# A two-block forward pass on one core: every norm split into its parts, and the end worked off by tiles of 128 tokens

## The chip, the cores and the metric

The kernel runs on one core of a Trainium2 chip. The metric is the device time of one execution in microseconds (us). Engines are named as in the profile: PE is the TensorE matmul engine (PEld its weight loads), DVE is VectorE, ACT is ScalarE, POOL is GpSimd, SP the engine that only issues DMAs.

## The reference

All is float32, for 512 tokens of width 1024. A first block runs on x, a second on the result. What touches the change are the norms between the products, and the end:

```python
def rms_norm(x, g):
    y = x * lax.rsqrt(jnp.mean(x * x, axis=-1, keepdims=True) + EPS)
    return y * g
# first block
h = rms_norm(x, g_pre_mix);  proj = h @ w_in                    # stage in1
mem_kv = rms_norm(mem, g_mem) @ w_mem_kv
y = concat(rms_norm(y_attn), rms_norm(y_conv), rms_norm(y_x)) @ w_out   # out1
x = x + rms_norm(y, g_post_mix)
f = square(relu(rms_norm(x, g_pre_mlp) @ w_up)) @ w_down        # up, down
x = x + rms_norm(f, g_post_mlp)
# second block: h = rms_norm(x) * (1 + scale) + shift; the same for 256 context rows
lat, ctx = h_lat @ w_in_2, h_ctx @ w_in_2                       # in2q, in2
q = rms_norm(lat[0]) @ w_q_b;  kv = rms_norm(lat[1], ctx[1]) @ w_kv_b   # mla0q ...
...                                  # attention, a gated scan, out, router
# expert layer: each token's 4 expert rows, weighed and added, then
x = x + gate * sum(prob[k] * expert_row[k] for k in range(4))
out = rms_norm(x, final_norm_g)
```

## The kernel before, in words

Activations lie transposed: the partitions hold 128 features, a tensor of width 1024 is eight chunks of 128 x 512 tokens. A product stage (`products`, L849) takes weight tiles of 1 MB that SP has queued, and works on pairs of output chunks: eight input chunks by eight matmuls of 512 columns, then ACT evacuates the pair from its banks (L1351). A float32 matmul is two records in the trace. There are only two sets of banks for pairs, so PE's third pair needs ACT to have emptied the first.

Each engine runs its own written-out program, in order, and waits on semaphores. A norm is a chain over four engines. DVE squares the chunks into two buffers `sq` (L1606), PE sums the squares over the partitions with a matrix of ones (`norm`, L910), ACT takes the root (`norm_root`, L1358), DVE inverts it (L1613), PE spreads the result over the partitions (`norm_spread`, L920), DVE multiplies chunk after chunk by it (L1619). Before the change PE's program holds sums and spread as one block between two product stages. Those blocks stand:

- ahead of `in1` for `pre_mix` and then `mem`; ACT's program goes on behind the root of `mem` with two sines for the rotary angles, a load of another function table and a sigmoid (L1393 to L1397), and only then evacuates `in1`. DVE computes the angles behind its own part of the norm of `mem`;
- ahead of `out1` for `attn`, `conv`, `xattn`, one after another; behind `out1` for `post_mix`, whose result is added to x chunk by chunk (L1730, L1731), and then for `pre_mlp`, whose squares DVE takes when all additions are done; likewise `post_mlp` and `mix2` behind `down`;
- between `in2q` and `in2` for `ctx`, behind `in2` for `qin`, `ckv_lat` and `ckv_ctx`, with the rotation of the keys, and then `mla0q`.

The expert layer runs 84 blocks of 32 rows: `up` L1238, `down` L1260, weight tiles of 1 MB queued on SP into 20 slots (two of them in the buffer of x), and a store of each block's 128 KB of results on ACT's queue. The last block stands in a loop of its own (`Fori`), since its count is only known at run time; ahead of it DVE waits for the store of the third block from the end, and then picks the last block's biases. During the expert layer x is kept in memory, since its buffer serves as weight slots; SP loads it back (`x<-x_kept`) when the last block's `down` is done. Then POOL gathers the expert rows by 16 indirect DMAs of 128 rows, four for each tile of 128 tokens (L811). DVE weighs and adds the four rows of a tile (L2030, L2033), PE transposes the sum (L1323), ACT copies it (L1584), DVE scales it and adds it to x (L2018, L2019). When all four tiles are in x the norm `final` runs over all of x, and SP stores eight chunks (L733).

## Time and profile before

| | |
|---|---|
| median of 3 runs | 3381.93 us (3380.32 to 3383.77) |
| the profiled execution's own time | 3386.95 us |
| its span | 3384.9 us, mean granted clock 0.93 |
| PE, PEld busy | 89%, 46% |
| DVE, ACT, POOL busy | 29%, 19%, 6% |
| DMA | 585 MB, 173 GB/s over the span |

The span runs from the first to the last event of the profiled execution; 2.05 us of its time lie around the span. The busy shares are means over the whole span. PE is at nine tenths in nearly all of the page's 40 slices; it is the stretches in which it isn't that the change is about.

### The profile page before, as it was taken

The page shows a single profiled execution, that of the slowest core. Times are in us where ns is not written, and L with a number is a line of the kernel's source. Part 1 is how long each engine was busy: PE and PEld are TensorE (multiplying, and loading weights), DVE is VectorE, ACT ScalarE, POOL GpSimd, SP SyncE. Part 2 cuts the span into 40 slices and gives each one's busy share as a digit, 9 for nine tenths or more (in the row PEclk, how much of TensorE's full clock was granted, in tenths as well). Part 3 has the DMA queues.
Part 4 walks back from the last instruction along what each step waited for, and adds up shares of the span by engine and source line. Part 5 has one row for each costly group of instructions (what it writes and reads, how often), then busy time and mean ns, then how long its engine had stood idle before and what let it go on. Part 6 is the DMA issues. An engine that isn't in the chain of part 4 may idle for free.

```text
span 3384.9 us, 45853 instructions
## 1 busy us (share of the span) xinstructions
PE 3014.4 (89%) x19729; PEld 1551.5 (46%) x19729; DVE 980.2 (29%) x1988; ACT 652.4 (19%) x1345; POOL 190.3 (6%) x180
## 2 busy tenths in 40 slices
PE   6899879999888999889999896799899999999993
PEld 3554434444344666555666664433333333333331
DVE  2244130000222221444445545411122121111124
ACT  1133000000001333344334332110111111111101
POOL 0000000000000000111111111110000000000002
PEclk9998889999888999899999998799999999999996
DMA  3134212211201011511011110398999979999695
GB/s 150 50 150 174 87 47 78 75 62 50 100 27 35 27 44 41 196 44 44 19 44 44 44 38 0 133 414 339 414 375 385 418 311 418 401 386 392 263 380 217
DMA packets 116909, 585.12 MB, mean 173 GB/s; under 512 B 10244, under 2 KB 21540, under 8 KB 69860
## 3 DMA queue, kind: packets, MB, share of 16 engines
q1 hardware_dynamic: 92752, 536.14, 40.0%
q10 hardware_dynamic: 17652, 24.25, 2.0%
q0 software_dynamic: 6304, 21.80, 1.8%
q8 instruction: 156, 2.56, 0.3%
q14 instruction: 45, 0.37, 0.0%
HBM read 551.58 MB, written 30.57 MB: 172 GB/s over the span
## 4 chain that ended last, share of the span: by engine, by line
PE 77%; DMA 10%; DVE 8%; ACT 2%; issue 1%; SPq 1%; ACTq 0%; POOL 0%; DVEq 0%; POOLq 0%
PE product_banks L849 37%; PE product_banks L1238 14%; PE product_banks L1260 8%; DMA space<-in_wgu 6%; PE score_banks L1132 3%; DMA x<-in_wgu 2%; PE out_bank L1000 1%; PE out_bank L920 1%; PE score_banks L937 1%; PE out_bank L959 1%; SPq L713 1%; PE turn_bank L910 1%; PE product_banks L1157 1%; DVE sq L1606 1%; PE product_banks L836 1%
## 5 line engine op out<-in xcount | busy, mean ns | idle before, releaser
L849 PE MATMUL product_banks<-space 128*128 128x512 f32 (+2 forms) x3888 | 1384.0, 508 | 32.3 <-DVE space L1832 13.4
L849 PEld LDWEIGHTS product_banks<-space 128*128 128x128 f32 x3888 | 687.2, 196 | 613.0 <-issue 552.2
L1238 PE MATMUL product_banks<-space 128*32 128x512 f32 x4848 | 581.5, 613 | 56.3 <-DMA space<-in_wgu 56.3
L1238 PEld LDWEIGHTS product_banks<-space 128*32 128x32 f32 x4848 | 141.0, 111 | 373.7 <-issue 266.6
L1260 PE MATMUL product_banks<-space,rstd 128*32 128x256 f32 x5024 | 300.7, 392 | 1.2 <-ACT rstd L1545 1.2
L1967 DVE TENSOR_TENSOR sq<-product_banks,cst 128x512 f32<-128x512 f32 x85 | 58.8, 692 | 755.4 <-PE product_banks L1238 755.4
L1351 ACT ACTIVATE space<-product_banks 128x512 f32<-128x512 f32 (+1 forms) x226 | 110.1, 523 | 796.1 <-PE product_banks L849 776.6
L1260 PEld LDWEIGHTS product_banks<-space,rstd 128*32 128x32 f32 x5024 | 168.4, 114 | 162.3 <-issue 73.4
L762 POOL TENSOR_TENSOR space<-space 128x512 f32<-128x512 f32 x112 | 132.0, 1193 | 1033.0 <-ACT space L1484 932.7
L1132 PE MATMUL score_banks<-space 128*128 128x64 f32 x896 | 126.3, 289 | 27.3 <-issue 21.1
L1132 PEld LDWEIGHTS score_banks<-space 128*128 128x128 f32 x896 | 124.6, 212 | 42.1 <-issue 38.3
L1606 DVE TENSOR_TENSOR sq<-space 128x512 f32<-128x512 f32 (+1 forms) x58 | 33.0, 605 | 375.5 <-PE turn_bank L910 237.9
L1541 ACT ACTIVATE ms<-sq 128x256 f32<-128x256 f32 x85 | 35.4, 417 | 459.3 <-DVE sq L1970 459.3
L910 PE MATMUL turn_bank<-sq,cst 128*32 128x128 f32 (+1 forms) x784 | 47.1, 337 | 79.8 <-DVE sq L1606 78.4
L1545 ACT ACTIVATE rstd<-turn_bank 128x256 f32<-128x256 f32 x85 | 32.7, 384 | 365.8 <-PE turn_bank L1249 365.8
L1238 PE MATMUL product_banks<-x,space 128*32 128x512 f32 x592 | 76.2, 628 | 7.1 <-DMA x<-in_wgu 7.1
L1853 DVE COPY_PREDICATED space<-cst,score_banks 128x256 f32<-128x256 uint8 x112 | 58.3, 520 | 67.7 <-PE score_banks L1132 67.0
L1738 DVE TENSOR_TENSOR space<-space 128x1024 f32<-128x1024 f32 x16 | 19.6, 1226 | 200.0 <-ACT space L1351 200.0
L1861 DVE TENSOR_TENSOR space<-space 128x256 f32<-128x256 f32 x112 | 69.5, 620 | 12.8 <-ACT space L1501 12.8
L784 POOL DMA_INDIRECT cst<-h_rows,space x21 | 20.0, 954 | 923.0 <-PE score_banks L1227 917.5
L910 PEld LDWEIGHTS turn_bank<-sq,cst 128*32 128x32 f32 x784 | 18.0, 124 | 115.0 <-DVE sq L1606 81.1
L1981 DVE TENSOR_TENSOR zeros<-product_banks,cst 128x256 f32<-128x256 f32 x84 | 35.7, 425 | 120.8 <-PE product_banks L1260 113.2
(300 smaller groups left out, 2476.3 us busy)
## 6 DMA issues: line engine op xcount, KB each, us to landing
space<-in_wgu SPq DMA_DIRECT2D x230, 1024.0 KB, 21.7
space<-in_wdn SPq DMA_DIRECT2D x116, 1024.0 KB, 21.9
space<-in_wt SPq DMA_DIRECT2D x104, 1024.0 KB, 5.1
x<-in_wgu SPq DMA_DIRECT2D x26, 1024.0 KB, 23.1
y_rows<-zeros ACTq DMA_DIRECT2D x2, 6400.0 KB, 29.5
x<-in_wdn SPq DMA_DIRECT2D x12, 1024.0 KB, 23.5
y_rows<-zeros ACTq DMA_DIRECT2D x84, 128.0 KB
space<-in_wt SPq DMA_DIRECT2D x13, 512.0 KB, 4.5
```

Of the source, the lines that this page charges most:

```text
L762: gp.tensor_tensor(dlt[:, L % 2, 0:T].rearrange("p (b s) -> p b s", s=2 * hf), c3, ref.broadcast_to([P, nb, 2 * hf]), ALU.subtract).then_i ...
L849: ins = nc.tensor.matmul(bank[0:rows, at:at + cols], lhsT, rhs, start=(i == 0), stop=(i == len(mm) - 1))
L910: ins = nc.tensor.matmul(PT[ROWS * q:ROWS * q + ROWS, 0:w // 4], ones[:, 0:ROWS], sq[:, g % 2, w // 4 * q:w // 4 * (q + 1)], start=(c == 0 ...
L1132: ins = nc.tensor.matmul(LB[L % 2][:, 64 * c:64 * c + 64], X[:, L % 2, cs_], half, start=True, stop=True)
L1238: ins = nc.tensor.matmul(bank[ROWS * g:ROWS * g + ROWS, :], xT_[:, k, :], w[:, 512 * g:512 * g + 512], start=(k == 0), stop=(k == DC - 1))
L1260: ins = nc.tensor.matmul(bank[ROWS * g:ROWS * g + ROWS, :], aT_[:, P * c + ROWS * d:P * c + ROWS * d + ROWS], w[:, c, 256 * g:256 * g + 25 ...
L1351: ins = nc.scalar.activation(dst, src, func, bias=bias, scale=scale)
L1606: V.tensor_tensor(sq[:, g % 2, 0:w], src[:, c, 0:w], src[:, c, 0:w], ALU.mult).then_inc(s_sq, 1)
L1853: V.copy_predicated(to, mk, LB[L % 2][:, 0:256].rearrange("p (c b s) -> p c b s", c=TT, s=hf)).then_inc(s_at, 1)
L1861: V.tensor_tensor(xv[:, :, qh], ev[:, :, qh], views(qq, hf)[:, :, qh], ALU.mult)
L1967: V.tensor_tensor(tbuf, bank, bias[:, 0:512], ALU.add).then_inc(s_u, 1)
L1981: V.tensor_tensor(to, bank, bias[:, 512:768], ALU.add).then_inc(s_y, 1)
```

## The change

**Norms.** `mem`'s sums and spread move into the stream of `in1` (behind 16 and 32 matmuls), `ctx`'s into that of `in2q`, `qin`'s into that of `in2`, those of `ckv_lat` and `ckv_ctx`, with the key rotation, into `mla0q` behind 18 matmuls. `attn`, `conv` and `xattn` are done abreast: all squares, all sums, all roots, all inversions, all spreads. A product stage behind a norm starts with the first chunk that is multiplied, not with the last. The squares of an output are summed within the stage that makes it (`products_and_sums`). The squares of `pre_mlp` and `mix2` are taken by ACT, chunk by chunk as DVE adds (`residual_squares`). x is loaded first, and the constants in two parts.

**x back.** `x<-x_kept` is queued ahead of the last block's tiles, which go to other slots.

**The end.** All 16 gathers have buffers of their own. For each tile ACT weighs the first row (`weigh_first`), DVE adds the second and third, and PE transposes that sum into a bank by a product with the identity and adds the fourth row there by a product with the identity times the row's weights. DVE adds the bank, times the gate, to x. The norm and the stores run per tile as well: ACT squares, PE sums with a full 128 x 128 matrix of ones (which also spreads), ACT takes the root and multiplies by the gain, DVE inverts and multiplies, SP stores 512 KB.

```diff
-            sp.dma_start(cst[:, :], consts).then_inc(s_const, 16)
+            sp.dma_start(x, xT).then_inc(s_in, 16)
+            sp.dma_start(cst[:, 0:2 * P], consts[:, 0:2 * P]).then_inc(s_unit, 16)
             sp.dma_start(vec[:, :], vecs).then_inc(s_const, 16)
-            sp.dma_start(x, xT).then_inc(s_in, 16)
+            sp.dma_start(cst[:, 2 * P:N_CONST], consts[:, 2 * P:N_CONST]).then_inc(s_const, 16)
...
+                for i in range(NS_SPACE, NS):
+                    sp.wait_ge(*released[i + NS * (loads_of_slot[i] - 1)])
+                sp.dma_start(x, xkept).then_inc(s_xback, 16)
...
-                sp.wait_ge(s_dn, n_more + N_FIXED_BLOCKS)
-                sp.dma_start(x, xkept).then_inc(s_xback, 16)
...
+                for i in range(TT):
+                    sp.wait_ge(s_fin, i + 1)
...
+            def products_and_sums(stage, name, source=None):
+                size = products_in(stages[stage][0])
+                for i, _ in enumerate(product_steps(stage)):
+                    if source and i < DC - 1:
+                        pe.wait_ge(s_norm, source + i + 1)
+                    p, done = divmod(i + 1, size)
+                    if p >= 2 and done == DC:
+                        norm_sum(name, 2 * p - 4)
+                        norm_sum(name, 2 * p - 3)
+                for c in range(4, DC):
+                    norm_sum(name, c)
...
-            norm("mem")
-            norm_spread("mem")
...
-            products("in1", "pre_mix")
+            for i, _ in enumerate(product_steps("in1")):
+                if i < DC - 1:
+                    pe.wait_ge(s_norm, normed("pre_mix", i + 2))
+                if i == 2 * DC - 1:
+                    norm("mem")
+                if i == 4 * DC - 1:
...
-            norm("attn")
-            norm_spread("attn")
-            norm("conv")
-            norm_spread("conv")
-            norm("xattn")
-            norm_spread("xattn")
-            pe.wait_ge(s_norm, normed("xattn"))
-            products("out1")
-            norm("post_mix")
+            for name in ("attn", "conv", "xattn"):
+                norm(name)
+            for name in ("attn", "conv", "xattn"):
...
-            products("in2q", "mix2")
-            norm("ctx")
-            norm_spread("ctx")
-            pe.wait_ge(s_norm, normed("ctx"))
-            products("in2")
-            norm("qin")
-            norm_spread("qin")
+            for i, _ in enumerate(product_steps("in2q")):
+                if i < DC - 1:
+                    pe.wait_ge(s_norm, normed("mix2", i + 2))
+                if i == 2 * DC - 1:
+                    norm("ctx")
+                if i == 4 * DC - 1:
+                    norm_spread("ctx")
+            for i, _ in enumerate(product_steps("in2")):
+                if i == 2 * DC - 1:
+                    norm("qin")
+                    pe.wait_ge(s_norm, normed("ctx"))
+                if i == 4 * DC - 1:
+                    norm_spread("qin")
             norm("ckv_lat")
-            norm_spread("ckv_lat")
             norm("ckv_ctx")
-            norm_spread("ckv_ctx")
-            pe.wait_ge(s_evac, stages["in2"][1])
-            rope(8)
-            pe.wait_ge(s_norm, normed("ckv_ctx"))
-            products("mla0q")
+            pe.wait_ge(s_norm, normed("qin"))
+            for i, _ in enumerate(product_steps("mla0q")):
+                if i == 17:
+                    norm_spread("ckv_lat")
+                    norm_spread("ckv_ctx")
+                    pe.wait_ge(s_evac, stages["in2"][1])
+                    rope(8)
+                    pe.wait_ge(s_norm, normed("ckv_ctx"))
             pe.wait_ge(s_evac, stages["mla0q"][1])
             rope(9)
             for g in range(4):
...
+            def sum_squares(i):
+                pe.wait_ge(s_fsq, i + 1)
+                if i:
+                    pe.wait_ge(s_frt, i)
+                for c in range(DC):
+                    ins = nc.tensor.matmul(PT[:, 0:P], ones, squares[:, i % 2, P * c:P * c + P], start=(c == 0), stop=(c == DC - 1))
+                ins.then_inc(s_fmm, 1)
...
+                bank = row_banks[i % 2]
+                pe.wait_ge(s_acc, 2 * i + 2)
+                if i >= 2:
+                    pe.wait_ge(s_xt, i - 1)
                 for c in range(DC):
-                    ins = nc.tensor.transpose(S[:, P * c:P * c + P], acc[:, i, P * c:P * c + P], ident)
-                ins.then_inc(s_tT, 1)
-            norm("final")
-            norm_spread("final")
+                    nc.tensor.matmul(bank[:, P * c:P * c + P], acc[:, i, P * c:P * c + P], ident, start=(c % 4 == 0), stop=False)
+                if i >= 2:
+                    sum_squares(i - 2)
+                j = TOPK * i + 3
+            sum_squares(TT - 2)
+            sum_squares(TT - 1)
...
+            def residual_squares(name, added):
+                for c in range(DC):
+                    g = chunk0[NI[name]] + c
+                    act.wait_ge(s_xadd, added + c + 1)
+                    act.wait_ge(s_mm, g - 1)
+                    nc.scalar.activation(sq[:, g % 2, :], x[:, c, :], F.Square).then_inc(s_sq, 1)
...
+            def weigh_first(i):
+                j = TOPK * i
+                act.wait_ge(*yg_landed(j))
+                nc.scalar.activation(acc[:, i, :], yg[:, j, :], F.Copy, scale=prob[:, j:j + 1]).then_inc(s_y0, 1)
+
+            act.wait_ge(s_weigh, 1)
+            for i in range(3):
+                weigh_first(i)
             for i in range(TT):
-                act.wait_ge(s_tT, i + 1)
-                nc.scalar.activation(yT[:, :, P * i:P * i + P], v3(S[:, :], DC), F.Copy).then_inc(s_tTc, 1)
-            norm_root("final")
+                ts = slice(P * i, P * i + P)
+                act.wait_ge(s_xt, i + 1)
+                if i >= 2:
+                    act.wait_ge(s_fmm, i - 1)
+                nc.scalar.activation(v3(squares[:, i % 2, :], DC), x[:, :, ts], F.Square).then_inc(s_fsq, 1)
+                if i == 0:
+                    weigh_first(3)
+                for c in range(DC):
+                    ins = nc.scalar.activation(fin[:, c, ts], x[:, c, ts], F.Copy, scale=vcol("final_norm_g_2", c))
+                ins.then_inc(s_gain, 1)
+                act.wait_ge(s_fmm, i + 1)
+                nc.scalar.activation(ms[:, ts], PT[:, 0:P], F.Sqrt, bias=const("eps"), scale=1.0 / D).then_inc(s_frt, 1)
...
+            def add_two(i):
+                dve.wait_ge(s_y0, i + 1)
+                for j in (TOPK * i + 1, TOPK * i + 2):
+                    dve.wait_ge(*yg_landed(j))
+                    if j % TOPK == 2:
+                        dve.wait_ge(s_acc, 2 * i + 1)
+                    V.scalar_tensor_tensor(acc[:, i, :], yg[:, j, :], prob[:, j:j + 1], acc[:, i, :], ALU.mult, ALU.add).then_inc(s_acc, 1)
+
+            def finish(i):
+                dve.wait_ge(s_frt, i + 1)
+                link(V.reciprocal(rstd[:, ts], ms[:, ts]))
+                dve.wait_ge(s_gain, i + 1)
```

PE's program at the start, before. The names are output and inputs; L910 sums squares, L920 spreads, L849 is `in1`; x counts matmuls.

```order
L910 MATMUL turn_bank<-sq,cst 32x128 x32
L920 MATMUL out_bank<-rstd,cst 128x128 x4
L910 MATMUL turn_bank<-sq,cst 32x64 x32
L920 MATMUL out_bank<-rstd,cst 128x64 x4
L849 MATMUL product_banks<-space 128x512 x64
L849 MATMUL product_banks<-space 128x256 x64
```

The same place after the change (L947 sums, L957 spreads, L874 is `in1`).

```order
L947 MATMUL turn_bank<-sq,cst 32x128 x32
L957 MATMUL out_bank<-rstd,cst 128x128 x4
L874 MATMUL product_banks<-space 128x512 x16
L947 MATMUL turn_bank<-sq,cst 32x64 x32
L874 MATMUL product_banks<-space 128x512 x16
L957 MATMUL out_bank<-rstd,cst 128x64 x4
L874 MATMUL product_banks<-space 128x512 x32
L874 MATMUL product_banks<-space 128x256 x64
```

The sums of `mem` stand behind the first pair of `in1`, its spread behind the second. ACT's program beside it, after the change, from its start; the row with `ms` and 64 is the root of `mem`, L1414 evacuates `in1`.

```order
L1423 ACTIVATE ms<-turn_bank,cst 128x128
L1423 ACTIVATE ms<-turn_bank,cst 128x64
L1466 ACT_TABLE_LOAD
L1466 ACTIVATE space<-space 128x512
L1468 ACTIVATE space<-space 128x512
L1470 ACT_TABLE_LOAD
L1470 ACTIVATE small<-vec 128x16
L1414 ACTIVATE space<-product_banks 128x512 x8
```

Nothing moved on ACT: no evacuation stands ahead of root, sines and sigmoid. The second place is PE's program from `in2` to `mla0q`, before.

```order
L849 MATMUL product_banks<-space 128x256 x8
L910 MATMUL turn_bank<-sq,cst 32x128 x24
L920 MATMUL out_bank<-rstd,cst 128x128 x4
L910 MATMUL turn_bank<-sq,cst 32x128 x8
L920 MATMUL out_bank<-rstd,cst 128x128 x4
L910 MATMUL turn_bank<-sq,cst 32x64 x8
L920 MATMUL out_bank<-rstd,cst 128x64 x4
L929 MATMUL score_banks<-space,cst 128x512
L849 MATMUL product_banks<-space 128x512 x20
```

And after the change.

```order
L947 MATMUL turn_bank<-sq,cst 32x128 x24
L874 MATMUL product_banks<-space 128x256 x16
L957 MATMUL out_bank<-rstd,cst 128x128 x4
L874 MATMUL product_banks<-space 128x512 x8
L874 MATMUL product_banks<-space 128x256 x8
L947 MATMUL turn_bank<-sq,cst 32x128 x8
L947 MATMUL turn_bank<-sq,cst 32x64 x8
L874 MATMUL product_banks<-space 128x512 x18
L957 MATMUL out_bank<-rstd,cst 128x128 x4
L957 MATMUL score_banks<-rstd,cst 128x64 x4
L966 MATMUL score_banks<-space,cst 128x512
```

Sums and spread of `qin` (x24, then x4) now have products of `in2` between them, and the two other norms have 18 matmuls of `mla0q`. The third place is DVE's program in the end, after the change: L2140 adds a gathered row, L2153 adds a tile to x, L2145 and L2147 finish a tile's norm.

```order
L2140 SCALAR_TENSOR_TENSOR space<-space 128x1024 x4
L2153 SCALAR_TENSOR_TENSOR x<-score_banks,mod,x 128x128 x8
L2140 SCALAR_TENSOR_TENSOR space<-space 128x1024 x2
L2153 SCALAR_TENSOR_TENSOR x<-product_banks,mod,x 128x128 x8
L2140 SCALAR_TENSOR_TENSOR space<-space 128x1024 x2
L2145 RECIPROCAL rstd<-ms 128x128
L2147 TENSOR_TENSOR space<-space,rstd 128x8x128
L2153 SCALAR_TENSOR_TENSOR x<-score_banks,mod,x 128x128 x8
L2145 RECIPROCAL rstd<-ms 128x128
L2147 TENSOR_TENSOR space<-space,rstd 128x8x128
L2153 SCALAR_TENSOR_TENSOR x<-product_banks,mod,x 128x128 x8
```

Before, four additions and two operations on x stood for each tile, and all of the norm behind the last; now a tile takes two additions, eight small ones and its own two steps of the norm.

## Rows read from the trace of the kernel before

**Rows 1.** Page, part 4: the chain that ended last, by engine.
```profile
PE 77%; DMA 10%; DVE 8%; ACT 2%; issue 1%; SPq 1%; ACTq 0%; POOL 0%; DVEq 0%; POOLq 0%
```

**Rows 2.** PE's waits over the span: waited for, us in total, times, longest us.
```profile
PE turn_bank L910 <- DVE sq L1606: 78.4, 46, 18.7
```

**Rows 3.** DMA issues of the span: KB each, median us to landing.
```profile
x<-x_kept SPq DMA_DIRECT2D x1, 2048.0 KB, 7.8
outT<-space SPq DMA_DIRECT2D x8, 256.0 KB, 2.2
cst<-in_consts SPq DMA_DIRECT2D x1, 1718.0 KB, 9.0
```

**Rows 4.** Timeline, 20 to 45 us: start, us, engine line op, idle before it.
```profile
27.93 5.35 DVE L1619 SCALAR_TENSOR_TENSOR space<-x,vec,out_bank 128x512 f32<-128x512 f32 x8 [2.17 <-PE out_bank L920]
```

**Rows 5.** ACT's timeline, 48 to 60 us.
```profile
51.00 1.28 ACT L1397 ACT_TABLE_LOAD   x1
...
56.45 1.08 ACT L1351 ACTIVATE space<-product_banks 128x512 f32<-128x512 f32 x2 [3.94 <-PE product_banks L849]
```

**Rows 6.** Chain in order of time, 0 to 690 us: start, us, what.
```profile
1.78 16.03 DMA x<-in_xT
...
40.40 84.86 PE product_banks L849 x256
...
460.93 221.82 PE product_banks L849 x512
```

**Rows 7.** Timeline, 346 to 373 us: the norms ahead of out1.
```profile
349.16 2.60 DVE L1606 TENSOR_TENSOR sq<-space 128x512 f32<-128x512 f32 x4
...
352.83 0.95 DVE L1613 RECIPROCAL rstd<-ms 128x128 f32<-128x128 f32 x1 [1.08 <-ACT ms L1358]
...
353.84 2.07 PE L920 MATMUL out_bank<-rstd,cst 128*128 128x128 f32 x8 [1.46 <-DVE rstd L1613]
...
372.55 1.22 PE L849 MATMUL product_banks<-space 128*128 128x512 f32 x1 [1.50 <-DVE space L1619]
```

**Rows 8.** Timeline, 449 to 457 us: the norm pre_mlp.
```profile
450.13 1.29 DVE L1606 TENSOR_TENSOR sq<-x 128x512 f32<-128x512 f32 x2
...
456.60 0.37 ACT L1358 ACTIVATE ms<-turn_bank,cst 128x128 f32<-128x128 f32 x1 [21.69 <-PE turn_bank L910]
```

**Rows 9.** Timeline, 982 to 1056 us: norms behind in2q and in2.
```profile
982.99 0.43 PE L910 MATMUL turn_bank<-sq,cst 128*32 128x64 f32 x16
...
995.65 33.61 PE L849 MATMUL product_banks<-space 128*128 128x512 f32 x96 [6.42 <-DVE space L1754]
...
1029.19 0.65 PE L910 MATMUL turn_bank<-sq,cst 128*32 128x128 f32 x16
...
1052.89 3.42 PE L849 MATMUL product_banks<-space 128*128 128x512 f32 x5
```

**Rows 10.** Timeline, 680 to 690 us: PE behind an idle stretch, at down.
```profile
685.17 5.40 PE L849 MATMUL product_banks<-space 128*128 128x512 f32 x8 [2.44 <-DVE space L1738]
```

**Rows 11.** Chain in order of time, 3280 to 3330 us.
```profile
3283.84 15.05 DMA y_rows<-zeros
...
3320.32 8.33 DMA y_rows<-conditions
```

**Rows 12.** Line 811 alone: the gathers, DMA to landing.
```profile
DMA to landing us min/median/max: 4.4/6.1/6.5
```

**Rows 13.** Groups of instructions, DVE by shape: busy us, mean ns.
```profile
L1642 DVE SCALAR_TENSOR_TENSOR space<-score_banks,cst 128x128 f32<-128x128 f32 x8 | 2.3, 291 | 3.9 <-PE score_banks L937 3.6
```

**Rows 14.** Timeline, 3349 to 3367 us: the end.
```profile
3350.00 1.77 POOL L811 DMA_INDIRECT space<-y_rows,space  x1 [0.30 <-issue]
...
3357.02 4.06 DVE L2033 SCALAR_TENSOR_TENSOR space<-space 128x1024 f32<-128x1024 f32 x3
...
3361.14 1.97 PE L1323 MATMUL score_banks<-cst,space 128*128 128x128 f32 x8 [5.38 <-DVE space L2033]
...
3363.14 1.02 ACT L1584 ACTIVATE space<-score_banks 128x1024 f32<-128x1024 f32 x1 [6.33 <-PE score_banks L1323]
```

## What I predict, and why

> **What bounds the kernel now.** I read the page from the busy shares and the slices to the chain that ended last, and then the waits. PE carries 77% of that chain, DMA 10%, DVE 8% [rows 1]: time is to be had where PE stands still or runs at half clock. The waits of PE name the place: it waits 78.4 us for DVE's squares, in 46 waits [rows 2]. A norm between two product stages keeps PE nearly idle, and the stage behind it begins at the lower level of the granted clock: the ordinary 512-column record takes 221.82 / 512 = 0.433 us [rows 6], the first eight of `down` take 5.40 us, 0.675 each [rows 10], the first of `out1` 1.22 [rows 7]. So one idle stretch costs about 5.40 - 8 x 0.433 = 1.9 us beside its own length. What bounds the end is in rows 14: the last gather is issued at 3350.0, it lands 6 us later [rows 12], and the span ends 28.9 us behind that, at 3384.9.
>
> **The start: 1 us lost.** x is issued at 1.78 and lands at 17.8, behind 1.7 MB of constants [rows 6]; those take 9.0 us [rows 3], so 2 MB first in the queue take 9.0 x 2048 / 1718 = 10.7 and land at about 11.4, 6.4 earlier. The first multiplication follows from 27.93 [rows 4] to 21.5, the first matmul of `in1` comes one chunk later, at 22.2, not at 40.40 [rows 6]. That is 18.2 us. What is given back: `mem`'s sums in the stream, 3.4 (a group of 16 such records takes 0.43 at full clock [rows 9] and there are four; I take twice that, for the gaps around each chunk's group), and its spread, 1.0 (half of the 2.07 of rows 7, at full clock). And a wait that the order of ACT's program makes. PE's third pair needs the first evacuated. On ACT the evacuation stands behind the root of `mem`, the two sines, the table load and the sigmoid, the sines wait for DVE's angles, and those stand behind DVE's norm of `mem`, which waits for the spread. The spread is now behind pair 1: 22.2 + 16.05 (40.40 to 56.45 for pair 0 [rows 5, 6]) + 3.4 + 32 x 0.433 + 1.0 is 56.5. From the spread's end to the sigmoid's it was 40.40 to 52.5 (the table load from 51.00 to 52.3 [rows 5], 0.2 for the sigmoid), with the evacuation's 1.08 it is 13.2 us, in which PE has nothing. It costs 2.0 of clock again. `in1` ends at 22.2 + 84.9 + 3.4 + 1.0 + 13.2 + 2.0 = 126.7 against 125.3: **-1.4**. The bounds are no such wait (+13.8), and a wait with 3 us more of slow records (-4).
>
> **Attn, conv, xattn: +10.7.** Before it is 349.16 to 372.55, 23.4 us [rows 7]. Now eight squares in a row, 0.65 each, to 354.4; the last sums and root 1; three inversions of 0.95 [rows 7], the first two beside the spreads; three spreads of 2.07 back to back end at about 363, where the attn chunks have long been multiplied, and `out1` starts: 9.5, and 1.2 of clock, since PE has just worked 6 us.
>
> **post_mix to pre_mlp, and post_mlp to mix2: +5.5 each.** DVE squares from 450.13 on, the root is at 456.60 [rows 8], 6.5 us. Now ACT squares each chunk while DVE multiplies the next, and behind the last addition stand one square and four matmuls: 1.0. The two have the same shape. The sums of post_mix within the stage may give up to 1.5 more each; none would be left if the additions waited for ACT. I take nothing for it.
>
> **ctx: +8.7.** It is 982.99 to 995.65, 12.7 us, and the 96 records behind it take 33.61 [rows 9] where 48 of 0.433 and 48 of half that make 31.2: 15.1 in all. In the stream it costs 3.4 for the sums, 1.0 for the spread, and some 2 of gaps.
>
> **qin and ckv: +12.** It is 1029.19 to 1052.89, 23.7 us [rows 9]. Now `qin`'s sums cost 3.7 (24 x 2 records, 0.65 for 16 [rows 9], and gaps), its spread 1.0, the ckv sums 1.7, their spreads and the rotation 3.4, and the restart 2: 11.8. What covers ACT's and DVE's part are the 18 matmuls of `mla0q` (15.6 us); if `qin` were late, PE would wait in front of them, up to 4.
>
> **x back ahead of the last block: +0.9.** The last block's tiles are now behind 2 MB: 7.8 less the 2.2 that even 256 KB take [rows 3], 5.6, less 1.2 that its last tile is asked for earlier: -4.4. Gained is the last store's landing, 8.33 beside the load of x [rows 11], about 3 alone: +5.3. The bounds: the store of which DVE waits ahead of the last block took 15.05 [rows 11] and may take more with the copy beside it (-4); the copy hidden beside stores gives +3. The Trainium skill (DMA: Bandwidth & Descriptors, Queues, rings and completion order) says that each DMA engine takes turns between queue rows packet by packet, so a small store on another queue should not stand behind all that SP has queued. The trace shows 15.05 us for 128 KB under load; the page would make this item about +1.5.
>
> **The end: +8.5.** The gathers keep their pace. Behind the last landing DVE owes the finish of tile 0, tile 2's addition, the finish of tile 1 and tile 3's addition, each about 2.3 (eight additions of 0.291 [rows 13]; 0.95 and 1.35), 9; then ACT's square 1.0 (as the copy of rows 14), the sums 2, root 0.4, inversion 0.95, multiplication 1.35 (a third of 4.06 [rows 14]) and a store of 512 KB, 3: 17.7, and about 2.7 between engines: 20.4 against 28.9. This wants PE at full clock. The matrices of a tile are three times 16 records; 8 of them took 1.97 us at half clock [rows 14], so a tile takes 12 us there, four tiles 47 from the second landing on, and the end comes some 18 later: **-9**. PE has more to do than before, and doesn't stop; I take the upper case, with both as bounds. The table load, 1.28 [rows 5], is once on the path in both kernels, and ACT goes on at once behind it. By the Trainium skill (ScalarE: Activation LUTs, What ACT_TABLE_LOAD costs) a switch costs 2.66 us with its drain; that would change the end by 1.4 at most.
>
> **The sum:** -1.4 + 10.7 + 5.5 + 5.5 + 8.7 + 12 + 0.9 + 8.5 = 50.4. The profiled execution has 3386.95 us, 2.05 more than its span and 5.0 more than the median; the change would take it to 3336.6. From the median of 3381.93 it is 3331.5, and I say **3332**.
>
> **Rivals.** (a) All as above, chance 0.60, own range 3322 to 3342. (b) No wait in `in1`, since the angles don't wait for the spread or the evacuation comes first: the start gains 13.8, 3317; against it stands the order of ACT's rows. 0.08. (c) The clock falls at each norm that now stands in a stream, and in the end: five places by 2 us and half of the end's 18, 18 to 20 us less: 3350. For it: the clock falls already at waits of some us [rows 10]. 0.17. (d) The two copies and the end give nothing, since DVE's additions are bound by the landings and the stores by the queue: 9.4 less, 3341. 0.12. (e) On the other side: after the short waits that each stage now has, the clock stays at its lower level for the product stages themselves. A 512-column record then takes 0.85 (1.22 and less were seen only in the first few [rows 7]); each costs 0.42 more, and 120 of them eat the 50 us, out of 3888. From 130 on it is slower. `in1`'s first pair, 32 records in 16.05 us [rows 5, 6], shows that such a stretch is possible; that it ends there speaks against it. 3385 to 3400, 0.02. The rest, 0.01, is no change.
>
> **How the numbers follow.** The unknown costs add to about 10 us either way: the end -17.5 or +2.5, the start +15, the copy -5 or +2, the others 4. The range 3314 to 3348 takes in (a), (b) and (d) and most of (c). A measurement of this kernel can tell 0.2%, 7 us, from no change. Faster by more: 0.97; within it: 0.01; slower: 0.02.
>
> **What the profile of the changed kernel would show.** Step one: `in1`'s first matmul near 22, PE idle for some 13 us near 57, until ACT's first evacuation near 70; right after a sigmoid. If that idle stretch is missing, (b) is right. Out1's first matmul is 14 us behind the first square of attn. PE has no idle stretch of 12 us between `in2q` and `mla0q`. The gap from the last addition of post_mix to the root of pre_mlp is near 1.5. The last store of a block lands 3 us after issue, the last block's `down` ends some 4 us later than its queue alone would have it. In the end PE's records of 128 columns take 0.12 us, not 0.25, and the span ends about 20 us behind the last landing. The prediction is wrong by most if the clock in the page's slices is lower than before in the middle of the stages, or if the PE of the end is at half.

## The result, and the profile after

The changed kernel takes 3329.39 us (median of 4 runs, 3322.44 to 3333.18) against 3381.12 for the kernel before beside it: the ratio is 0.9847, 95% interval 0.9834 to 0.9859, or 52 us less. The profiled execution has 3331.52 us and a span of 3329.8, 55.1 below that of before. Here is the page after: the span, PE's busy time, and the chain that ended last by engine.

```profile
span 3329.8 us, 46098 instructions
...
PE 3017.5 (91%) x19817; PEld 1561.9 (47%) x19817; DVE 952.9 (29%) x1975; ACT 681.7 (20%) x1408; POOL 188.9 (6%) x180
...
PE 79%; DMA 9%; DVE 6%; ACT 3%; another core or an unknown queue 1%; issue 1%; ACTq 0%; SPq 0%; POOL 0%; DVEq 0%; POOLq 0%
```

PE's share of the chain rose from the 77% of [rows 1] to 79%, DVE's fell from 8% to 6%. The waits of PE after (waited for, us in total, times, longest) answer to [rows 2].

```profile
PE product_banks L874 <- ACT space L1414: 19.4, 8, 13.1
...
PE turn_bank L947 <- ACT sq L1430: 14.7, 16, 2.2
...
PE turn_bank L947 <- DMA cst<-in_consts: 13.5, 1, 13.5
...
PE turn_bank L947 <- DVE sq L1706: 9.9, 23, 1.8
```

Of the 78.4 us of waiting for DVE's squares 9.9 are left, and 14.7 for the squares that ACT now takes. Two long waits are to be read beside them: a new one of 13.1 us for ACT to empty the product banks, and one of 13.5 us for constants at the start.

**Where the time went.** A product stage's evacuations on ACT are the same in number and order in both kernels, so the difference of their start times is a running balance. It makes this table (us; in the balance minus is earlier than before; "this part" is what the stretch up to that place gained, minus is a loss; of the 85 expert blocks 84 stand ahead of the loop).

| place | before | after | balance | this part | forecast |
|---|---|---|---|---|---|
| in1, last pair emptied | 125.28 | 131.23 | +5.95 | -5.95 | -1.4 |
| out1, last pair | 429.41 | 425.36 | -4.05 | +10.0 | +10.7 |
| up, first pair | 476.77 | 465.26 | -11.51 | +7.5 | +5.5 |
| in2q, first pair | 955.63 | 934.20 | -21.43 | +9.9 | +5.5 |
| in2, first pair | 1012.08 | 979.68 | -32.40 | +11.0 | +8.7 |
| mla0q, once spreads and rotation are done | 1071.36 | 1025.70 | -45.66 | +13.3 | +12 |
| last block but one, up done | 3287.43 | 3236.93 | -50.50 | +4.8 | 0 |
| first gather | 3329.56 | 3280.87 | -48.69 | -1.8 | +0.9 |
| end of the span | 3384.9 | 3329.8 | -55.1 | +6.4 | +8.5 |

**The start.** The timeline of the changed kernel, 10 to 75 us (start, us, engine line op, in brackets the idle time before it and what ended it).

```profile
13.51 1.08 PE L947 MATMUL turn_bank<-sq,cst 128*32 128x128 f32 x16 [13.51 <-DMA cst<-in_consts]
...
19.29 1.28 ACT L1423 ACT_TABLE_LOAD   x1 [19.29 <-PE turn_bank L947]
...
24.91 16.99 PE L874 MATMUL product_banks<-space 128*128 128x512 f32 x32 [0.84 <-DVE space L1724]
...
58.85 1.00 PE L957 MATMUL out_bank<-rstd,cst 128*128 128x64 f32 x8
...
59.89 3.22 DVE L1724 SCALAR_TENSOR_TENSOR space<-space,vec,out_bank 128x256 f32<-128x256 f32 x8 [13.84 <-PE out_bank L957]
...
69.29 0.63 ACT L1466 ACTIVATE space<-space 128x512 f32<-128x512 f32 x1 [22.52 <-DVE space L1793]
69.82 0.61 ACT L1468 ACTIVATE space<-space 128x512 f32<-128x512 f32 x1
70.45 1.28 ACT L1470 ACT_TABLE_LOAD   x1
71.75 0.21 ACT L1470 ACTIVATE small<-vec 128x16 f32<-128x16 f32 x1
71.87 2.04 ACT L1414 ACTIVATE space<-product_banks 128x512 f32<-128x512 f32 x4
...
72.99 2.93 PE L874 MATMUL product_banks<-space 128*128 128x512 f32 x3 [13.13 <-ACT space L1414]
```

PE starts at 13.51, released by the constants and not by x, which DVE squares from 10.51 on. ACT's first table load, 1.28 us, comes only at 19.29, behind the last sum, so that the root of `pre_mix` stands 1.3 us later behind the sums than before. In the kernel before it ran at the very start, beside the loads:

```profile
0.87 1.28 ACT L1358 ACT_TABLE_LOAD   x1 [0.87 <-PEq L2131]
```

The changed program has ACT wait for the constants ahead of this root; that this is what put the load there is likely, but no run tests it. PE reaches `in1` at 24.91 and spreads `mem` at 58.85. Then the chain can be read downward: DVE applies the norm of `mem` (59.89), computes the angles, ACT takes the sines (69.29), loads a table (70.45), runs the sigmoid (71.75), and only then empties the first pair (71.87), which had been ready since 41.9. PE's third pair starts at 72.99 after 13.13 us of idle time. That answers to [rows 5], where the same rows stood before PE had need of them.

**The three norms ahead of out1.** The chain in order of time, 355 to 375 us.

```profile
363.19 2.08 PE out_bank L957 x8
365.26 3.41 PE score_banks L957 x16
368.68 6.60 PE product_banks L874 x15
```

The three spreads stand back to back and `out1` starts right behind them, 13.0 us behind the first square (355.68) where it was 23.4 [rows 7].

**Squares on ACT.** The timeline at `pre_mlp`: the last square, the root, `up`.

```profile
442.51 0.63 ACT L1430 ACTIVATE sq<-x 128x512 f32<-128x512 f32 x1 [0.75 <-PE turn_bank L947]
...
443.92 0.37 ACT L1423 ACTIVATE ms<-turn_bank,cst 128x128 f32<-128x128 f32 x1 [0.78 <-PE turn_bank L947]
...
448.31 4.63 PE L874 MATMUL product_banks<-space 128*128 128x512 f32 x5 [0.84 <-DVE space L1724]
```

DVE's last addition ends at 442.5, the root comes 1.4 us later, where the squares alone took 6.5 [rows 8]. At `post_mlp`:

```profile
898.20 0.37 ACT L1423 ACTIVATE ms<-turn_bank,cst 128x128 f32<-128x128 f32 x1 [1.87 <-PE turn_bank L947]
...
899.61 1.16 PE L957 MATMUL out_bank<-rstd,cst 128*128 128x128 f32 x8 [1.47 <-DVE rstd L1717]
```

The root is 3.0 us behind the evacuation of 895.24, not 4.9, and the spread takes 1.16 us, not the 2.07 of [rows 7]: PE has hardly stopped, and its clock is still up.

**Norms in the stream.** The timeline from 934 to 1000 us, `ctx` and `qin`.

```profile
937.28 14.00 PE L874 MATMUL product_banks<-space 128*128 128x512 f32 x32
...
951.12 1.00 PE L957 MATMUL out_bank<-rstd,cst 128*128 128x64 f32 x8
...
983.15 8.86 PE L874 MATMUL product_banks<-space 128*128 128x256 f32 x32
...
991.85 1.05 PE L957 MATMUL out_bank<-rstd,cst 128*128 128x128 f32 x8
```

Each spread is 1.0 us between products that run on, behind `ctx` at 0.44 a record of 512 columns; what stood between the stages in [rows 9] is not there. Behind the sums of `qin` the 32 records of 256 columns take 8.86 us, in e7, e11 and e12 7.17: here the clock did fall in the stream, for 1.7 us.

**The copies and the end.** DMA issues over the span (KB each, us to landing), which answer to [rows 3]:

```profile
x<-in_xT SPq DMA_DIRECT2D x1, 2048.0 KB, 9.6
...
cst<-in_consts SPq DMA_DIRECT2D x1, 128.0 KB, 12.1
```

x lands after 9.6 us, but the 128 KB of constants queued behind it only after 12.1. And the end, from the store of the last block:

```profile
3276.59 1.09 ACTq L1631 DMA_DIRECT2D y_rows<-conditions  x1
3280.12 0.18 POOL L806 TENSOR_TENSOR space<-space 1x1 f32<-1x1 f32 x1 [111.31 <-DMA y_rows<-conditions]
...
3316.11 1.95 PE L1370 MATMUL turn_bank<-space,cst 128*128 128x128 f32 x16
3317.05 2.15 DVE L2153 SCALAR_TENSOR_TENSOR x<-product_banks,mod,x 128x128 f32<-128x128 f32 x8
...
3319.24 1.06 ACT L1678 ACTIVATE space<-x 128x1024 f32<-128x1024 f32 x1 [0.77 <-DVE x L2153]
...
3320.35 2.85 PE L1370 MATMUL turn_bank<-space,cst 128*128 128x128 f32 x16 [2.29 <-ACT space L1678]
...
3324.62 1.23 DVE L2147 TENSOR_TENSOR space<-space,rstd 128x1024 f32<-128x1024 f32 x1
```

POOL goes on 3.5 us after the store is issued, not 8.3 [rows 11]. Tile 3 is added at 3317.05, squared at 3319.24, and its sums take 2.85 us for 16 records, where those of tile 2 just ahead (3316.11) take 1.95: the granted clock fell once more. The last two windows of the span show where it stood (busy us and count by engine, granted clock, DMA share, GB/s).

```profile
3281.00:3300.00 19.00, 8.97 (x62) 8.81 (x63) 6.27 (x9) 3.44 (x3) 14.62 (x15) 0.66 0.90 332
3300.00:3330.00 30.00, 17.71 (x133) 17.03 (x131) 20.81 (x40) 17.18 (x42) 0.95 (x1) 0.80 0.42 140
```

### The profile page after: what moved, and what is told of

Read it like the earlier page. It is cut to its first block, busy times and chain, and to the rows that moved or that the text cites. A ratio compares the mean times of both kernels' runs of the same rounds, so it can differ in the third digit from the quotient of the medians.

```text
span 3329.8 us, 46098 instructions
## 1 busy us (share of the span) xinstructions
PE 3017.5 (91%) x19817; PEld 1561.9 (47%) x19817; DVE 952.9 (29%) x1975; ACT 681.7 (20%) x1408; POOL 188.9 (6%) x180
## 4 chain that ended last, share of the span: by engine, by line
PE 79%; DMA 9%; DVE 6%; ACT 3%; another core or an unknown queue 1%; issue 1%; ACTq 0%; SPq 0%; POOL 0%; DVEq 0%; POOLq 0%
PE product_banks L874 37%; PE product_banks L1284 14%; PE product_banks L1306 8%; DMA space<-in_wgu 6%; PE score_banks L1178 3%; DMA x<-in_wgu 2%; PE out_bank L1037 1%; PE score_banks L974 1%; PE out_bank L996 1%; PE product_banks L1203 1%; PE turn_bank L947 1%; PE product_banks L861 1%; PE out_bank L957 1%; DMA space<-in_wdn 1%
## 5 line engine op out<-in xcount | busy, mean ns | idle before, releaser
L874 PE MATMUL product_banks<-space 128*128 128x512 f32 (+2 forms) x3888 | 1383.4, 508 | 39.0 <-ACT space L1414 19.4
L874 PEld LDWEIGHTS product_banks<-space 128*128 128x128 f32 x3888 | 686.1, 196 | 614.0 <-issue 547.4
L1284 PE MATMUL product_banks<-space 128*32 128x512 f32 x4864 | 583.8, 614 | 55.3 <-DMA space<-in_wgu 52.4
L1414 ACT ACTIVATE space<-product_banks 128x512 f32<-128x512 f32 (+1 forms) x226 | 109.9, 522 | 767.0 <-PE product_banks L874 745.3
L947 PE MATMUL turn_bank<-sq,cst 128*32 128x128 f32 (+1 forms) x720 | 39.6, 315 | 39.5 <-ACT sq L1430 14.7
L1582 ACT ACTIVATE space<-space 128x256 f32<-128x256 f32 x112 | 47.3, 423 | 118.6 <-DVE space L1980 118.6
L2099 DVE TENSOR_TENSOR zeros<-product_banks,cst 128x256 f32<-128x256 f32 x84 | 35.7, 425 | 121.5 <-PE product_banks L1306 112.6
```

Of the source, the lines that this page charges most:

```text
L874: ins = nc.tensor.matmul(bank[0:rows, at:at + cols], lhsT, rhs, start=(i == 0), stop=(i == len(mm) - 1))
L947: ins = nc.tensor.matmul(PT[ROWS * q:ROWS * q + ROWS, at:at + w // 4], ones[:, 0:ROWS], sq[:, g % 2, w // 4 * q:w // 4 * (q + 1)], start=( ...
L1284: ins = nc.tensor.matmul(bank[ROWS * g:ROWS * g + ROWS, :], xT_[:, k, :], w[:, 512 * g:512 * g + 512], start=(k == 0), stop=(k == DC - 1))
L1414: ins = nc.scalar.activation(dst, src, func, bias=bias, scale=scale)
L1582: nc.scalar.activation(ev[:, :, qh], dv[:, :, qh], F.Exp)
L2099: V.tensor_tensor(to, bank, bias[:, 512:768], ALU.add).then_inc(s_y, 1)
```

## Experiments

All times below are medians, with the ratio to the kernel before from the same chip and its 95% interval. The changed kernel's own profiled execution stood at a lower clock in some stretches than those of the experiments, so that most of them are up to 3 us ahead of it at places that their edit does not touch; at the end of `in1` the seven that leave the start alone are 0.1 to 2.3 us ahead. So a difference of that size counts for nothing by itself: a balance is read across the stage that was edited, and where that isn't enough, by the rows at the place. The medians of e7, e8 and e12 lie 5.7 to 6.1 us above that of the changed kernel, where the balance moves by 9.5 to 11.2 at the edited stage; where the rest goes isn't resolved.

**e1: pairs of in1 emptied ahead of the sines.**

```diff
             norm_root("mem")
+            evacuate_to(stages["in1"][0] + 2)
             act.wait_ge(s_ang, 1)
```

> The changed kernel, but ACT empties the first two pairs of in1 ahead of the sines, the table load and the sigmoid. If PE's 13.3 us of idle time behind the spread of mem come from that order, they go, and with them some 2 us of half clock behind them: in1 ends 13 to 15 us earlier and the time is about 3315 (ratio to before 0.980 to 0.981). If PE would wait there anyway, for a weight tile or for DVE, the time stays at 3329 within 3 us.

Measured: 3310.77 us, ratio 0.9792 (0.9776 to 0.9808). The timeline at the place:

```profile
58.50 1.09 ACT L1414 ACTIVATE space<-product_banks 128x512 f32<-128x512 f32 x2 [12.61 <-PE product_banks L874]
...
59.14 16.10 PE L874 MATMUL product_banks<-space 128*128 128x512 f32 x37
```

ACT empties pair 1 at 58.50, PE's products start 0.6 us after and don't stop (37 records in 16.10, 0.435 each). `in1` ends 16.8 us earlier than in the changed kernel, and at the end of `out1` it is 18.0. The wait is ACT's order. By the rows it costs 13.3 us between the two records beside it, and 2.9 of half clock behind it (the first eight records take 6.38 us in the changed kernel and 3.48 here); the other 0.5 arises ahead of it, in `in1`'s first records, where the edit changes nothing.

**e2: angles ahead of the norm of mem.** DVE's eleven instructions for the angles stand ahead of `norm("mem", hm, "g_mem")`; ACT is as in the changed kernel.

```diff
-            dve.wait_ge(s_tok, 16)
-            norm("mem", hm, "g_mem")
             dve.wait_ge(s_pos, 16)
             link(V.tensor_copy(cosT, ang.bitcast(i32)))
...
             V.tensor_scalar(trn, trn, PI, -PI, ALU.min, ALU.max).then_inc(s_ang, 2)
+            dve.wait_ge(s_tok, 16)
+            norm("mem", hm, "g_mem")
```

> The changed kernel, but DVE computes the rotary angles ahead of its part of the norm of mem, so that sines and sigmoid do not stand behind the spread; ACT's order is as in the changed kernel. If the link from the spread over DVE's angles to the sines makes the wait, it goes here as fully as by the other order on ACT: 3315. If ACT's order alone matters, whatever DVE does (table loads and sines behind the root of mem), some 2 to 5 us of the wait stay: 3317 to 3320.

Measured: 3308.86 us, 0.9779 (0.9762 to 0.9797); the first evacuation is at 49.25 instead of 71.87, `in1` ends 16.3 us earlier. Breaking the chain at either link removes all of it.

**e3: the first constants ahead of x.**

```diff
-            sp.dma_start(x, xT).then_inc(s_in, 16)
             sp.dma_start(cst[:, 0:2 * P], consts[:, 0:2 * P]).then_inc(s_unit, 16)
+            sp.dma_start(x, xT).then_inc(s_in, 16)
```

> The changed kernel, but the first 256 columns of the constants are loaded ahead of x, not behind it. PE waited for them until 13.5 us, when x had been there since 10.5. They are 128 KB; x should land about 0.5 us later and PE start at about 11.5: 2 us less, all of it on the path, 3327 (the timing alone may not tell that, the time of the first matmul will). If small loads are late because of the other loads that start at once, and not because of their place, the first matmul stays near 13.5 and nothing is gained.

Measured: 3321.55 us, 0.9822 (0.9805 to 0.9838). The first rows of DVE and PE:

```profile
11.18 1.29 DVE L1706 TENSOR_TENSOR sq<-x 128x512 f32<-128x512 f32 x2 [9.79 <-DMA x<-in_xT]
...
12.02 1.17 PE L947 MATMUL turn_bank<-sq,cst 128*32 128x128 f32 x16 [12.02 <-DVE sq L1706]
```

x lands 0.7 later (11.18), PE starts 1.5 earlier, and `in1` starts 1.5 earlier (23.41; 24.6 to 25.0 in the others that load x first). That is what the edit is worth. The balance of 1.8 to 2.1 at the evacuations doesn't show more, since executions without the edit are up to 2.3 ahead there. The place in the queue is what counted. The time fell by 8 us; that surplus lies in the stretches that differ between any two profiled executions, and I don't put it down to the edit.

**e4: mem ahead of in1 again.**

```diff
             norm_spread("pre_mix")
+            norm("mem")
+            norm_spread("mem")
             pe.wait_ge(s_norm, normed("pre_mix", 1))
...
-                if i == 2 * DC - 1:
-                    norm("mem")
-                if i == 4 * DC - 1:
-                    norm_spread("mem")
```

> The changed kernel, but sums and spread of mem stand ahead of in1 again, as in the kernel before. in1 starts about 12.5 us later, near 37, sums and spread (4.3 us) and the 13.3 us of waiting go from its stream, and with them 2 us of half clock: in1 ends 7 to 9 us earlier than with mem in the stream, 3321. If the wait for ACT were there in either place, in1 would end 12 us later than in the changed kernel: 3341.

Measured: 3316.48 us, 0.9799 (0.9778 to 0.9821); `in1` ends 11.0 us earlier, 9.5 at the end of `out1`. Undone, this part is faster than done. Against e1, which keeps `mem` in the stream, it loses 5.8 us at the one place and 8.5 at the other.

**e5: x loaded back last.**

```diff
-                for i in range(NS_SPACE, NS):
-                    sp.wait_ge(*released[i + NS * (loads_of_slot[i] - 1)])
-                sp.dma_start(x, xkept).then_inc(s_xback, 16)
...
+                sp.wait_ge(s_dn, n_more + N_FIXED_BLOCKS)
+                sp.dma_start(x, xkept).then_inc(s_xback, 16)
                 for i in range(TT):
                     sp.wait_ge(s_fin, i + 1)
```

> The changed kernel, but x is loaded back as before, when the last block's down is done, behind its tiles. By the prediction the copy ahead of the block was worth 0.9 us, so this is 0.9 slower. By the trace of the changed kernel the last block's up ends 4.7 us later against the blocks ahead of it, its down 6.8, and the last store lands 4.8 earlier: undone it is 1.8 to 2 us faster. In the trace: last store near 8 us to landing instead of 3.5, and the last block's first addition 4.7 earlier. The timing can hardly tell either; the trace's boundaries can.

Measured: 3326.33 us, 0.9838 (0.9824 to 0.9852), against the changed kernel unclear. The parts can be read. The expectation compared two executions in which the stream of weight tiles stood one tile (2.7 us) apart against PE, though the code of the expert layer is the same: with the copy first, `up` of the last block is done 28.0 to 28.2 us behind that of the block ahead of it in six of the profiled executions, 24.7 to 26.0 in six others. The phase shows elsewhere too: the six others and the kernel before lose 2.6 to 3.3 us between expert blocks 76 and 78 that the first six don't lose, and e5 doesn't, so it belongs with the first six. Like with like: from `up` of the block ahead to the last store 39.7 us with the copy first, 35.7 with it last (and 37.3 in e1 against 32.9 before, in the other phase). That is 4.0 to 4.4 us. From the store to the first gather 4.3 against 9.4: 5.1. The copy's place is worth +1.2 to +0.5 us from `up` to the first gather. The expectation here was wrong, the prediction right.

**e6: tiles before finishes, on PE and DVE.**

```diff
+                if i == 3:
+                    sum_squares(0)
...
+            for i in range(1, TT):
+                sum_squares(i)
...
-            finish(0)
             add_tile(2)
-            finish(1)
+            finish(0)
             add_tile(3)
+            finish(1)
```

> The changed kernel, but in the end PE turns tile 3's sum ahead of the squares of tile 0 and sums the squares of tile 1 behind tile 3's fourth row, and DVE adds tiles 2 and 3 to x one finish earlier each. In the changed kernel tile 3's addition starts at 3317.05, 0.8 us after PE is done with it, and PE is done late since it sums squares before. If DVE and PE together bound the end, the last store is issued about 2 us earlier, the end is 2 us shorter from the first gather on (46.9 instead of 48.9). If the end is bound by the landings of the rows, nothing changes.

Measured: 3329.02 us, 0.9843 (0.9829 to 0.9858). From the first gather to the end 46.9 us, in the ten executions with the end as changed (the changed kernel, e1 to e5, e7, e8, e11, e12) 45.7 to 48.9, median 46.6. Nothing gained, and neither of the two explanations holds: the rows (ACT, DVE, ACT) show a third.

```profile
3304.75 0.37 ACT L1685 ACTIVATE ms<-turn_bank,cst 128x128 f32<-128x128 f32 x1 [3.17 <-PE turn_bank L1370]
...
3307.28 2.15 DVE L2153 SCALAR_TENSOR_TENSOR x<-product_banks,mod,x 128x128 f32<-128x128 f32 x8
...
3312.12 1.05 ACT L1678 ACTIVATE space<-x 128x1024 f32<-128x1024 f32 x1
```

Tile 3 is added 32.3 us behind the first gather (36.2 in the changed kernel, 34.0 in e8), but ACT squares the next tile only behind the root and the gains of the last one: the squares of tile 3 begin at 3312.12, 2.7 us after its addition has ended. And ACT is late at its first root (3304.75) since the edit itself makes PE sum tile 0's squares behind tile 3's sum: it waits 3.17 us there, and from then on squares, gains and root of the other three tiles follow one another without a break, 3.55 us for each.

**e7: ctx between the stages again.** The root stands behind all of `in2q`'s evacuations, too.

```diff
-                if i == 2 * DC - 1:
-                    norm("ctx")
-                if i == 4 * DC - 1:
-                    norm_spread("ctx")
+            norm("ctx")
+            norm_spread("ctx")
+            pe.wait_ge(s_norm, normed("ctx"))
```

> The changed kernel, but the norm of ctx stands between in2q and in2 again, as a block. The prediction said 8.7 us for this part; the two traces, by the evacuations of in2q and in2, say 11.0. So it is slower by 8.7 or by 11: 3338 or 3340. If the two figures differ because the clock's level behind the block was not what it was, the trace shows it in the first records of in2.

Measured: 3335.35 us, 0.9863 (0.9846 to 0.988). At the first pair of `in2` it has lost 11.2 us (its balance against the changed kernel goes from -0.2 to +11.05), at the second 9.4 is left, and in the expert layer 6.4 to 9.2 from its tenth block on. The part is worth 11, and 6 to 9 of it stays.

**e8: squares by DVE.**

```diff
-            residual_squares("pre_mlp", 0)
-            residual_squares("mix2", DC)
...
-            inverse_root("pre_mlp")
+            norm_stats("pre_mlp")
...
-            inverse_root("mix2")
+            norm_stats("mix2")
```

> The changed kernel, but DVE squares the new x for pre_mlp and for mix2 itself, behind its additions; all else (sums of the output within its stage, the shift on ACT) as changed. By the prediction the squares on ACT are worth 5.5 us each, 11 in all: 3340. If the 8.6 to 9.1 us that these two gaps lost come mostly from the squares, more than 14 is given back; I expect 5.7 each from the rows (last addition to root 7.1 before, 1.4 now), 11.4.

Measured: 3335.13 us, 0.9865 (0.9848 to 0.9882). The balance moves by 4.2 us at `pre_mlp` and 5.9 at `mix2`, 10.1.

**e9: the fourth row by DVE.**

```diff
-                for j in (TOPK * i + 1, TOPK * i + 2):
+                for j in (TOPK * i + 1, TOPK * i + 2, TOPK * i + 3):
...
-                pe.wait_ge(*yg_landed(j))
-                for c in range(DC):
-                    ins = nc.tensor.matmul(bank[:, P * c:P * c + P], yg[:, j, P * c:P * c + P], weigh[:, i, :], start=False, stop=(c % 4 == 3))
```

> The changed kernel, but the fourth row is added by DVE like the second and third, and PE only transposes the sum; the rest of the end stays by tiles. It gives DVE 1.34 us more for each tile and takes 16 records, 2.0 us, from PE. If DVE bounds the end, from the first gather to the end it takes 47.5 instead of 46.2 (the median of the eight profiled executions with this end); if PE does, 44. The rest of the run is not touched.

PE also turns the sum by 8 records a tile instead of 16 here (`transpose` in place of the product with the identity), so that it loses 24 records a tile and not 16.

Measured: 3330.61 us, 0.984 (0.9825 to 0.9856). From the first gather to the end 48.1 us, 1.5 more than the median of the ten executions with the changed end, but within their 45.7 to 48.9. So a gain, the 44 us of the case that PE bounds the end, is excluded; a loss isn't shown by one execution. The windows of its end, and of e2's, which has the changed end:

```profile
3282.00:3301.00 19.00, 3.91 (x16) 3.13 (x16) 9.75 (x15) 3.44 (x3) 15.01 (x14) 0.50 0.88 308
3301.00:3330.00 29.00, 12.02 (x80) 11.15 (x80) 22.19 (x39) 17.25 (x42) 2.99 (x3) 0.74 0.47 160
```

```profile
3260.00:3279.00 19.00, 8.56 (x60) 8.41 (x61) 8.09 (x13) 4.40 (x4) 14.77 (x14) 0.64 0.88 309
3279.00:3306.00 27.00, 16.09 (x134) 15.09 (x132) 19.08 (x36) 16.02 (x42) 2.65 (x3) 0.97 0.52 172
```

DVE does 32 us of work, not 27, and PE, with 80 records instead of 134 in the last stretch, runs at a granted clock of 0.74, not 0.97. Over the last 29 us of the ten executions with the changed end it is 0.80 to 0.96, and in the kernel before, with 104 records in the whole end, 0.50. So with less work PE stood at a lower clock; what that costs in time isn't shown, since DVE's own 5 us more lie beside it.

**e11: sums of the outputs behind their stages.**

```diff
-                    if p >= 2 and done == DC:
-                        norm_sum(name, 2 * p - 4)
-                        norm_sum(name, 2 * p - 3)
-                for c in range(4, DC):
+                for c in range(DC):
                     norm_sum(name, c)
```

> The changed kernel, but all squares of the outputs of out1 and down are summed behind the stage, not within it. I had taken nothing for that part; the traces say that from the last evacuation to the root it was 5.1 and 4.9 us and is 3.0, that the spread behind it then still runs at the upper clock (1.6 and 1.2 us instead of 2.07), and that the sums cost 1.5 in the stream. So 1 to 2.5 us are given back in the two places together: 3330 to 3332, and in the trace the first additions of post_mix and post_mlp come 0.5 to 1.3 us later each. If nothing was gained by it, the boundaries stay within 0.3.

Measured: 3329.87 us, 0.9838 (0.9823 to 0.9853). The stages without sums are 1.5 us shorter each; at `up` 1.9 of it is given back again, at `in2q` 3.8. So the part is worth 0.4 at `post_mix` and 2.3 at `post_mlp`. The rows at `post_mlp`:

```profile
896.29 0.37 ACT L1420 ACTIVATE ms<-turn_bank,cst 128x128 f32<-128x128 f32 x1 [4.06 <-PE turn_bank L944]
...
897.69 2.08 PE L954 MATMUL out_bank<-rstd,cst 128*128 128x128 f32 x8 [1.48 <-DVE rstd L1714]
```

The root is 5.2 us behind the evacuation of 891.14, and the spread takes 2.08 us, at half clock. Behind `qin`'s sums this execution gets 1.7 back without an edit there:

```profile
982.84 7.17 PE L874 MATMUL product_banks<-space 128*128 128x256 f32 x32
```

**e12: attn, conv, xattn one after another.**

```diff
             for name in ("attn", "conv", "xattn"):
                 norm(name)
-            for name in ("attn", "conv", "xattn"):
                 norm_spread(name)
```

On DVE, which the cut doesn't show, squares and inversion of each norm stand together again, and each root waits for its own sums alone.

> The changed kernel, but attn, conv and xattn are normed one after another again, each with its squares, sums, root, inversion and spread; out1 still starts as soon as its first input chunk and the last spread are there. Before, from the first square to the last spread's end it took 21.9 us, in the changed kernel 13.0 to the first matmul: 8.9 more, and 1 to 2 of half clock in out1's first records behind the longer idle stretch. So 9 to 11 us slower, 3339. The prediction had 10.7 for the part with the later start of out1. If the three chains had hidden each other already, less than 5.

Measured: 3335.45 us, 0.9869 (0.9852 to 0.9885). The first square and the first record of `out1`:

```profile
355.10 2.60 DVE L1705 TENSOR_TENSOR sq<-space 128x512 f32<-128x512 f32 x4
...
376.67 8.81 PE L874 MATMUL product_banks<-space 128*128 128x512 f32 x18
```

21.6 us lie between them, against 13.0; the balance moves by 9.5 us.

**e10: the best of it.** e1, e2 and e3 together, e6's order on DVE, on PE the squares of tile 0 summed ahead of tile 2's fourth row (in e6 ahead of tile 3's), and this on ACT (the root of a tile behind the squares of the next):

```diff
                 if i == 0:
                     weigh_first(3)
+                else:
+                    root(i - 1)
```

> All that helped together: first two pairs of in1 emptied ahead of the sines, angles ahead of the norm of mem, the first constants ahead of x, and another order of the end: DVE adds tiles 2 and 3 to x ahead of the finishes of tiles 0 and 1, PE puts the fourth row of tile 3 ahead of the squares of tile 1, and ACT squares the next tile before it takes the root of the last, since in the run with only PE and DVE reordered ACT's squares stood behind its roots and gains. The start should give 17 to 18 (one of the two orders) and 2 (the constants), 3309; the end 2 more: 13.1 us of DVE behind the last addition of two rows, from the first gather to the end 44 instead of 46.2. So 3307 (ratio 0.978). If the end is bound otherwise, 3309.

Measured: 3306.62 us, 0.9779 (0.9766 to 0.9793), 78 us below the kernel before (3384.7 beside it). From the first gather to the end it takes 45.1 us. The rows show tile 3 added and the last step of DVE. ACT's squares of tile 2 (3284.90) now stand beside that addition.

```profile
3284.83 2.15 DVE L2159 SCALAR_TENSOR_TENSOR x<-product_banks,mod,x 128x128 f32<-128x128 f32 x8
...
3293.80 1.22 DVE L2153 TENSOR_TENSOR space<-space,rstd 128x1024 f32<-128x1024 f32 x1
```

Tile 3 is added 31.0 us behind the first gather, but from there to the end of the last multiplication it is 10.2 us (8.8 in the changed kernel), a chain of ACT and DVE by turns, with all three finishes in it. The new end is 1.5 us below the median of the ten and 0.6 below the shortest of them, in one execution; the rest of the gain is the start. Against e2 alone (ratio 0.9779 as well) the total can't be told apart.

## Why the prediction was right

The time forecast was 3332 (3314 to 3348), the measured one is 3329.4. The mechanisms forecast are the ones seen, but that the sum came out within 3 us is partly luck: the start came 4.5 us worse than forecast, the parts around the two added norms and `ctx` 8.7 better in the table, 4.8 arose where nothing was forecast, and the end of the profiled execution came 2.1 worse.

- **The start** was forecast -1.4 and is -5.95. The mechanism was right, to the row: idle time 13.13 us where 13.2 stood in the sum, ended by the evacuation behind the sigmoid. What was mis-sized lies around it. `in1` came at 24.9 and not at 22.2: x landed 0.9 earlier than in the sum, but PE was held until 13.5 us by the 128 KB of constants queued behind x, 2.2 beyond what x alone asks (e3 gives 1.5 of it back), and the table load of 19.29 adds 1.3; neither was in the sum. The half clock behind the wait was put at 2.0; the eight records behind it take 5.6 to 6.4 us in the nine executions that have the wait and 3.5 in e1 and e2, so it is 2.1 to 2.9, at the upper end in the changed kernel's own profile. `in1`'s first 16 records took 0.8 longer there than before (9.96 against 9.20; in eight other executions 8.4 to 9.9). Rival (b), no wait, is excluded by the row.
- **attn, conv, xattn**: forecast 10.7; the balance gives 10.0, from which 1.5 for `post_mix`'s sums in `out1`'s stream are already taken, and e12 shows 9.5. Right.
- **post_mix to pre_mlp, post_mlp to mix2**: forecast 5.5 each, measured 7.5 (6.0 with the 1.5 that its sums cost in `out1`) and 9.9. The squares were right in their sum (e8: 4.2 and 5.9, 10.1 against 11). The step that failed is "I take nothing for it" for the sums within the stage: e11 shows 0.4 and 2.3. The rest was not in the sum at all: DVE no longer waits for each of its own additions and adds a chunk every 1.39 us, not every 1.51 (1 us for eight), and the first pair of `down` is 1.7 earlier, since its first eight records take 3.54 us and not 5.23. e12 has 5.23 again without an edit there: the clock's level in single stretches.
- **ctx**: forecast 8.7, measured 11.0, in e7 11.2. In the stream sums and spread cost 3.4 and 0.9, as forecast; the 2 us of gaps that I added were not there. In e7 1.7 of it is given back at once, since the records behind `qin`'s sums then run at full clock (7.17 us, not 8.86).
- **qin and ckv**: forecast 12, measured 13.3, without an experiment of its own. By the balance `qin`'s sums cost 5.5 and not 3.7, 1.7 of it the half clock of the 8.86 above, which is rival (c) in small; the restart of 2 us behind the ckv sums was not there (36 records in 15.72 us, 0.437 each).
- **x back**: forecast -4.4 + 5.3, measured -4.0 to -4.4 and +5.1. The 1.8 us of loss in the table is the phase of the tile stream: the kernel before stands in the one phase, the changed kernel's profile in the other, which gains 2.7 between blocks 76 and 78 and pays it in the last block. By the Trainium skill (DMA: Bandwidth & Descriptors, Queues, rings and completion order) each DMA engine takes turns between the queues by packets. I drew +1.5 from that without a working, and it was not sound: if turns kept a small store from paying, moving the copy would have gained it nothing. The last store's 9.4 us beside the copy (e5) and 4.3 without it show a small store that does pay for what another queue carries.
- **The end**: forecast 8.5, which makes 46.8 us from the first gather to the end; the median of the ten executions is 46.6, 8.7 less than the 55.3 before. In the profiled one the clock stood at 0.80 in the last 30 us and it took 48.9. That lies between the two bounds, and is rival (c) in small; rival (d), nothing from the end, is excluded, since all ten are 6 us or more below before. No run undoes the end as a whole. The Trainium skill (ScalarE: Activation LUTs, What ACT_TABLE_LOAD costs) gives 2.66 us for a switch with its drain; here the cosine ends at 70.43, the load takes 1.28 us from 70.45 and the sigmoid starts at 71.75. The whole switch takes 1.32 us between two busy instructions, and the trace shows no drain on either side.
- **The rest**, 4.8 us between `mla0q` and the last blocks, was forecast at 0. No instruction changed there. 2.7 of it is the phase of the tile stream, which the last block takes back; 2.1 remain. Single records take twice as long here and there, in other places in each execution; which of it the change brings can't be told from one profile each. Rival (e) did not happen: the mean granted clock rose from 0.93 to 0.941.

## What to carry to other kernels

When work is moved into a stream of another engine's work, read the programs of the engines between: whoever must free a buffer for the stream may stand, in its own order, behind a chain that waits for the moved work. Put buffer-freeing work ahead of such chains. An idle stretch costs more than its length: TensorE came back at half its clock, 2.1 to 2.9 us behind a wait of 13 and 1.7 to 1.9 behind short ones. And read a change that shifts everything after it by a running balance at marks that both kernels share, but take several executions of the same code first: here they differ by up to 2.3 us at the end of `in1` alone, and only what goes beyond that, or shows in the rows at the place, belongs to the edit.

## What the runs showed that I had not expected

- The half clock behind 13.1 us of idle PE costs 2.1 to 2.9 us, little more than the 1.9 behind 2.4 us of it [rows 10].
- ACT's table load moved from the start of the run, where it cost nothing, to behind the last sum, where it costs 1.3 us, though at that root the change touches nothing but a wait.
- In the end less work for PE went with a lower clock: 0.74 with 80 records in the last 29 us of e9, 0.80 to 0.96 with 128 to 155 in those of the ten executions with the changed end.
- 128 KB queued behind 2 MB took 12.1 us to land, 2.5 us more than those 2 MB's 9.6; ahead of them they cost x 0.7 us.
- The stream of weight tiles stands in one of two phases against PE, some 2.7 us apart, under the same code of the expert layer; what one phase gains ahead of the last block the last block takes back.
